# Block 1's run-up reordered, values formed by units, memory halves behind the turns

## The chip, the cores and the metric

The kernel runs on one core of a Trainium2 chip. The metric is the device time of one execution in microseconds (us), as the median of several runs.

## The reference

Two transformer blocks of two layers each work on one sequence of 256 tokens of width 1024, in float32. Cut to what matters here:

```
block 1, layer l (SWA = sliding window with sinks, DSA = sparse attention by an index):
  h = x @ w_in; qa,ka,va,qb,kb,vb,qi,ki,wi = split(h)     # 8 heads of 64; index: 8 heads of 32
  rope(qa, ka, qb, kb, qi); ki = rope(layer_norm(ki))
  idx = sum_h relu(qi_h . ki) * wi_h, causal; sel = top_k(idx, 64)
  oa = softmax(qa.ka/8 in a band of 128, with a sink) @ va
  ob = softmax(qb.kb/8 over sel and causal) @ vb
  x = layer_norm(a*x + [oa,ob] @ w_o); then a gated FFN with an extra input p, and a layer norm
block 2, layer l (MLA = latent attention, SLC = selected, WIN = window, with a compressed branch):
  three sets of causal attention, 8 heads each; x = layer_norm(a*x + mix @ w_out)
  cross attention with memory: k, v = (norm(mem) @ wkv) split; then a convolved FFN, layer norm
```

## The kernel before

The kernel is written by hand: each engine has one list of instructions (its queue), and semaphores make one wait for another. Tokens are two tiles of 128 (t = 0, 1). Big products are made from weights split in a high and a low part (ScalarE copies `whi`, L1348; VectorE, here DVE, subtracts to `wlo`, L1736) and three TensorE (PE) matmuls (L742 to L744). `token_stage` (PE) and `evict` (ScalarE) run a projection pass by pass: pass (q, t) is weight tile q for token tile t, and a dictionary names work that is put ahead of a pass (`before`) or behind one (`behind`).

In block 1 the input projection has seven weight tiles. Between its passes stand the turns (transposes through PE) of the index heads (`first_heads`), the index scores of tile 0 (`first_scores`, L1039), and on DVE the rotations (`rope`, L1800 to L1805) and the weighted sum of the index scores (`index_sum`, L2031) of rectified scores (ScalarE, L1519). GpSimd (POOL) rotates tile 0 of the window heads (L2421 to L2430). Behind the projection PE makes the index scores of tile 1, the turns of head groups 2 to 7 (`head_turns`, L1031), evicted by ScalarE (`heads_out`, L1509), and `attention` begins.

The sparse selection finds the 64 largest of a row in 8 rounds of 8 (`MAX8` L2111 and `MATCH_REPLACE8` L2113), for tile 0 on 128 columns and for tile 1 on 256, then builds a mask (L2116, L2118). DVE's function `top` makes these in the first six steps of attention.

`attention` works in steps i over half units. A unit is one kind of attention for one token tile, a half unit four of its heads. Block 1 has 4 units (8 half units, 11 steps): SWA t0, SWA t1, DSA t0, DSA t1. Block 2 has 6 (12 half units, 15 steps): MLA t0, t1, SLC t0, WIN t0, SLC t1, WIN t1. In step i:

- PE: the scores of half unit i (L898); a filler of block 2; a memory half, if step i is a slot (`SLOTS1`, `SLOTS2`); the values of half unit i-3 (L927, wait for `pt_ready`); the turns of the probabilities of half unit i-2 (L944, wait for `prob_ready`).
- DVE: mask and maximum of i (L1822, the CUSTOM rows, to L1835); the reciprocal for i-1 (L1847); `top(i)`; in even steps the low part of a finished unit's mix (L1861).
- ScalarE (ACT): in even steps the high part of the mix (L1437), the exponentials of i (L1452), the store of the step's memory half (`memory_store`, L1424), the evictions of the turned probabilities of i-2 (L1468), and in `HI_STEPS` a weight split.
- POOL: probabilities of half unit i-1 times the reciprocals (L2403).

A memory half (`memory_half`, L874 or L876) is 8 float32 matmul pairs of a product that block 2's cross attention needs later. It uses one PSUM bank, so each waits for the store of the one before (`kv_staged`). Six halves stand in each attention. When the second half of a tile is done, its room in the ring of weights is free, and the SyncE queue (SP) issues the next weight load.

Of the kernel before, what the change touches and what calls it, by code (L numbers as in the profile page):

```python
# [11 lines left out]
ALU = mybir.AluOpType  # L12
# [3 lines left out]
P = 128  # L16
S = 256
NT = S // P
# [29 lines left out]
SLOTS1 = (1, 2, 3, 5, 7, 9)  # L48
# [177 lines left out]
def build(nc, w, c, out):  # L226
# [52 lines left out]
    with ExitStack() as ctx:  # L279
# [124 lines left out]
        icomb_done = sem("icomb_done")  # L404
# [76 lines left out]
        relu = sy[:, 1, :].rearrange("p (h k) -> p h k", h=H)  # L481
# [173 lines left out]
        head_groups = [(10, 11), (12,), (5, 6), (7, 8), (9,), (0, 1), (2, 3), (4,)]  # L655
        n_const_dmas, n_param_dmas = len(const_dmas), len(param_dmas)
# [77 lines left out]
        def _(pe):  # L734
# [143 lines left out]

            def memory_between(n, banks):

                for half in range(2):
                    memory_half(n + half, banks[:, 2 + half, 0:TC])

            def attention(block, l, qT, kT, v, first_values=lambda t: None, filler=lambda step: None):
# [3 lines left out]
                for i in range(first, first + count + 3):  # L888
# [15 lines left out]
                    n = memory_slot(block, l, i - first)  # L904
                    if n is not None:
                        if n:
                            pe.wait_ge(kv_staged, n)
                        memory_half(n)
                    if half_ahead:
                        filler(i - first)  # L910
                    if i - 3 >= first:
                        n = i - 3
# [20 lines left out]
                    if first <= i - 2 < first + count:  # L933
# [5 lines left out]
                        for q, (b, a, kb) in enumerate(blk):  # L939
# [6 lines left out]
                            if q % 4 == 3:  # L946
                                ins.then_inc(pt_done, 1)

# [61 lines left out]
            for l in range(L):  # L1010
# [16 lines left out]
                def head_turns(q):  # L1027

                    for j, b in enumerate(head_groups[q]):
                        for t in range(NT):  # L1030
                            ins = pe.transpose((psa if q < 2 else psw)[:, q % 4, j * S + t * P:j * S + (t + 1) * P],  # L1031
# [40 lines left out]

                def bank_free(g, t):
                    if g < 2:
                        pe.wait_ge(pp_ready, 4 * l + 2 * t + g + 1)
                    else:
# [5 lines left out]
                             (6, 0): first_scores})  # L1082
                pe.wait_ge(relu_done, NT * l + 1)
                index_scores(1)

                pe.wait_ge(proj_ready, 8 * (l + 1))
                for q in range(2, 8):
                    if q == 2:
                        pe.wait_ge(qkb_roped, NT * (l + 1))
                    if q == 5:  # L1090
                        for t in range(NT):
                            pe.wait_ge(qka_roped[t], l + 1)
                    if q >= 6:
                        pe.wait_ge(heads_ready, 8 * l + q - 3)
                    head_turns(q)
                pe.wait_ge(heads_ready, 8 * (l + 1))
                pe.wait_ge(relu_done, NT * (l + 1))
# [1388 lines left out]
```

## Time and profile before

| | us |
|---|---|
| median of 3 runs | 1553.19 (1549.77 to 1553.95) |
| the profiled execution's own time | 1555.47 |
| its span | 1553.7 |
| busy: PE / PE weight load / DVE / ACT / POOL | 1497.1 / 1264.5 / 1063.1 / 778.6 / 123.3 |
| block 1's attention with its head turns, layers 0 and 1 | about 67 to 122 and 400 to 454 |
| block 2's attention, layers 0 and 1 | about 769 to 834 and 1199 to 1262 |

The profile is of one execution. Busy time is the time in which an engine had work in flight; matmuls are pipelined, so a busy PE need not be PE at its peak. All times of rows count from the start of the span.

### The profile page before, as it was taken

The numbers are of one execution on the slowest core, as the hardware profiler recorded it, in microseconds if no ns is written. First come the engines' busy times: TensorE is split into PE (matmuls) and PEld (weight loads), VectorE is DVE, ScalarE is ACT, GpSimd is POOL, SyncE is SP. The second block draws the span as 40 slices with busy tenths as digits, with TensorE's granted clock in tenths as the row PEclk, the third lists the DMA queues.
The fourth block names the chain that finished last, engine by engine and source line by source line (L and its number), as shares of the span: only waits on it lengthen the run. The fifth ranks groups of instructions, "written<-read, shape, count | busy, mean of one in ns | idle before, by whom it ended". The sixth has DMA issues, their size and how long they took to land.

```text
span 1553.7 us, 21682 instructions
## 1 busy us (share of the span) xinstructions
PE 1497.1 (96%) x8433; PEld 1264.5 (81%) x8433; DVE 1063.1 (68%) x1713; ACT 778.6 (50%) x1162; POOL 123.3 (8%) x98
## 2 busy tenths in 40 slices
PE   8989999999899999999999999999999999999997
PEld 5767888888777888878877988888788779888886
DVE  7767588667866787676345566878864455677777
ACT  4564444434464444433655344666545653446563
POOL 0130000000220000011022000000010320000000
PEclk9999999999999999999999999999999999999999
DMA  7624655655334755654614745556536147355551
GB/s 257 199 99 139 201 192 190 211 179 192 117 120 155 242 192 188 219 173 135 190 59 151 252 134 171 185 189 217 175 122 193 53 150 258 125 168 185 189 189 67
DMA packets 184429, 265.03 MB, mean 171 GB/s; under 512 B 7368, under 2 KB 139398, under 8 KB 184200
## 3 DMA queue, kind: packets, MB, share of 16 engines
q1 hardware_dynamic: 178712, 258.38, 50.1%
q10 hardware_dynamic: 5616, 5.26, 1.0%
q8 instruction: 68, 1.11, 0.3%
q14 instruction: 33, 0.27, 0.1%
HBM read 258.38 MB, written 5.24 MB: 170 GB/s over the span
## 4 chain that ended last, share of the span: by engine, by line
PE 77%; DVE 13%; ACT 5%; issue 2%; DVEq 2%; POOL 1%; ACTq 0%; POOLq 0%; DMA 0%; SPq 0%
PE psw L815 18%; PE psw L814 8%; PE psw L742 8%; PE psw L744 7%; PE psw L743 7%; DVE wlo L1736 5%; PE psa L742 4%; PE psa L744 4%; PE psa L743 4%; PE psa L874 3%; PE psa L876 3%; PE psa L927 2%; PE psw L898 2%; ACT sy L1452 1%; PE psa L944 1%
## 5 line engine op out<-in xcount | busy, mean ns | idle before, releaser
L1736 DVE TENSOR_TENSOR wlo<-raw,whi 128x2048 fp32r<-128x2048 f32 (+3 forms) x199 | 449.9, 2266 | 125.0 <-ACT whi L1348 124.5
L815 PE MATMUL psw<-xboth,whi 128*128 128x512 f32 x1344 | 464.8, 396 | 1.2 <-DVE wlo L1736 1.2
L1348 ACT ACTIVATE whi<-raw 128x2048 fp32r<-128x2048 f32 (+3 forms) x199 | 375.2, 1886 | 175.8 <-PE psw L744 91.3
L814 PE MATMUL psw<-xboth,wlo 128*128 128x256 f32 x1176 | 327.9, 279 | 0.0
L815 PEld LDWEIGHTS psw<-xboth,whi 128*128 128x128 f32 x1344 | 242.7, 188 | 49.1 <-DVE wlo L1736 2.3
L814 PEld LDWEIGHTS psw<-xboth,wlo 128*128 128x128 f32 x1176 | 221.7, 189 | 7.5
L742 PE MATMUL psw<-whi,xboth 128*128 128x512 f32 (+3 forms) x472 | 182.1, 386 | 5.3 <-DVE wlo L1736 5.3
L744 PE MATMUL psw<-whi,xboth 128*128 128x512 f32 (+3 forms) x472 | 178.9, 379 | 0.0
L743 PE MATMUL psw<-wlo,xboth 128*128 128x512 f32 (+3 forms) x472 | 178.9, 379 | 0.0
L1410 ACT ACTIVATE r<-psw 128x512 f32<-128x512 f32 x88 | 52.5, 596 | 174.6 <-PE psw L815 164.0
L742 PE MATMUL psa<-whi,rr 128*128 128x512 f32 x352 | 137.5, 391 | 1.4 <-DVE rr L2366 1.4
L743 PE MATMUL psa<-wlo,rr 128*128 128x512 f32 x352 | 137.0, 389 | 0.0
L2391 POOL TENSOR_TENSOR rstd<-vare,mhalf 128x1 f32<-128x1 f32 x26 | 36.7, 1414 | 1095.6 <-DVE vare L1758 1086.9
L2345 DVE SCALAR_TENSOR_TENSOR r<-r,pcol 128x254 f32<-128x254 f32 (+1 forms) x176 | 77.3, 481 | 57.9 <-ACT r L1702 53.9
L742 PEld LDWEIGHTS psw<-whi,xboth 128*128 128x128 f32 x472 | 88.9, 188 | 22.3 <-DVE wlo L1736 6.3
L744 PEld LDWEIGHTS psw<-whi,xboth 128*128 128x128 f32 x472 | 88.9, 188 | 15.9
L743 PEld LDWEIGHTS psw<-wlo,xboth 128*128 128x128 f32 x472 | 88.9, 188 | 15.2 <-issue 0.2
L744 PE MATMUL psa<-whi,rr 128*128 128x512 f32 x256 | 99.6, 389 | 0.0
L1903 DVE TENSOR_TENSOR r<-psw,r 128x512 f32<-128x512 f32 x88 | 60.6, 688 | 57.0 <-ACT r L1410 56.9
L1452 ACT ACTIVATE sy<-sy,nmx 128x256 f32<-128x256 f32 (+1 forms) x160 | 70.6, 446 | 22.9 <-DVE nmx L1835 22.8
L1702 ACT ACTIVATE r<-r,pcol 128x256 f32<-128x256 f32 x88 | 48.2, 596 | 67.3 <-DVE r L1903 67.3
L2403 POOL TENSOR_TENSOR sy<-sy,rden 128x512 f32<-128x512 f32 (+1 forms) x40 | 62.8, 1570 | 210.7 <-DVE rden L1847 169.8
(290 smaller groups left out, 2210.1 us busy)
## 6 DMA issues: line engine op xcount, KB each, us to landing
raw<-in_w_gu SPq DMA_DIRECT2D x44, 1024.0 KB, 5.1
raw<-in_ffn_w_up SPq DMA_DIRECT2D x42, 1024.0 KB, 5.1
raw<-in_w_down SPq DMA_DIRECT2D x22, 1024.0 KB, 4.9
raw<-in_ffn_w_down SPq DMA_DIRECT2D x22, 1024.0 KB, 4.9
raw<-in_w_in SPq DMA_DIRECT2D x20, 1024.0 KB, 5.3
raw<-in_xa_wkv SPq DMA_DIRECT2D x16, 1024.0 KB, 5.3
raw<-in_w_o SPq DMA_DIRECT2D x8, 1024.0 KB, 5.1
raw<-in_w_out SPq DMA_DIRECT2D x8, 1024.0 KB, 5.2
```

The source lines that it names most:

```text
L742: pe.matmul(o, lh, rh, start=first, stop=False)
L743: pe.matmul(o, lh, rl, start=False, stop=False)
L744: return pe.matmul(o, ll, rh, start=False, stop=last)
L814: pe.matmul(bank[:, 0:S], wl[:, k, cols], xhi[:, k, :], start=False, stop=False)
L815: ins = pe.matmul(bank.rearrange("p (i s) -> p i s", i=2), wh[:, k, cols], xboth[:, :, k, :], start=k == 0, stop=k == KD - 1)
L1348: nc.scalar.activation(tile_flat("hi", i), tile_flat("raw", i), ACT.Copy).then_inc(hi_ready, 1)
L1410: nc.scalar.activation(low_part[:, i], psw[:, 2 * i:2 * i + 2, S:2 * S], ACT.Copy).then_inc(low_out, 1)
L1452: ins = nc.scalar.activation(soft[:, u % 2, h, 0:nk], soft[:, u % 2, h, 0:nk], ACT.Exp, bias=nmx[:, u % 2, h:h + 1], scale=1.0, accum_out= ...
L1736: v.tensor_tensor(tile_flat("lo", i), tile_flat("raw", i), tile_flat("hi", i).bitcast(F32), ALU.subtract).then_inc(lo_ready, 1)
L1903: v.tensor_tensor((gsum, usum)[i].rearrange("p (c s) -> p c s", c=2), psw[:, 2 * i:2 * i + 2, 0:S], low_part[:, i], ALU.add).then_inc(ffn_ ...
L2345: ins = v.scalar_tensor_tensor(out=o, in0=whole[:, ch * S:(ch + 1) * S - lag], scalar=pcol[:, 1 + 2 * l, cc:cc + 1], in1=o, op0=ALU.mult, ...
L2403: g.tensor_tensor(x, x, rd.unsqueeze(3).broadcast_to([P, 2, 2, nk]), ALU.mult).then_inc(prob_ready, 1)
```

## The change

- The index scores go one pass earlier: those of tile 0 ahead of pass (5, 1), those of tile 1 (`second_scores`) ahead of pass (6, 0), into a rectified buffer of their own in `cblocks`; ScalarE's `rectified` moves with them.
- Behind the projection PE turns head groups 2 to 4, makes memory half 0 of the layer (slot -1), and then turns groups 5 to 7. ScalarE stores that half between the evictions of groups 4 and 5. The turns use other banks (`head_banks`).
- DVE makes four of tile 0's eight selection rounds ahead of attention: two behind the sum of tile 0, two behind the sum of tile 1. `TOP_STEPS` spreads the rest evenly over steps 0 to 5.
- In both blocks the values of both half units of a unit stand together in an even step (i-4 and i-3), where the first stood one step earlier.
- In both blocks a step's memory half stands behind the turns of the step, where it stood ahead of the values; step 1 of block 2 stays as it was. ScalarE stores it behind its evictions.

```diff
-SLOTS1 = (1, 2, 3, 5, 7, 9)
+SLOTS1 = (-1, 1, 3, 5, 7, 9)
+TOP_FIRST = 4
+TOP_STEPS = {0: (0, 4, 6), 1: (0, 6, 8), 2: (1, 0, 2), 3: (1, 2, 4), 4: (1, 4, 6), 5: (1, 6, 8)}
...
+        relus = [sy[:, 1, :].rearrange("p (h k) -> p h k", h=H), cblocks[:, 0:2048].rearrange("p (h k) -> p h k", h=H)]
...
+        head_banks = [(psa, 0), (psa, 1), (psw, 0), (psw, 2), (psw, 1), (psw, 3), (psa, 0), (psa, 1)]
...
+            def half_in_step(n):
+
+                if n:
+                    pe.wait_ge(kv_staged, n)
+                memory_half(n)
...
                     half_ahead = block == 2 and i - first == SLOTS2[0]
                     if not half_ahead:
                         filler(i - first)
-                    n = memory_slot(block, l, i - first)
-                    if n is not None:
-                        if n:
-                            pe.wait_ge(kv_staged, n)
-                        memory_half(n)
+                    half_now = memory_slot(block, l, i - first)
                     if half_ahead:
+                        half_in_step(half_now)
                         filler(i - first)
-                    if i - 3 >= first:
-                        n = i - 3
+                    for n in (i - 4, i - 3) if i % 2 == 0 and i - 4 >= first else ():
                         u, hf = divmod(n, 2)
...
+                    if not half_ahead and half_now is not None:
+                        half_in_step(half_now)
...
+                def second_scores():
+                    pe.wait_ge(relu_done, NT * l + 1)
+                    index_scores(1)
...
                 token_stage(1, "in", l, 7, x_in, 3, 0, bank_free,
                             {(2, 0): lambda: norm_turns(x_in, 1), (3, 0): param_turns,
                              (4, 0): memory_turns, (5, 0): first_heads,
-                             (6, 0): first_scores})
-                pe.wait_ge(relu_done, NT * l + 1)
-                index_scores(1)
-
+                             (5, 1): first_scores, (6, 0): second_scores})
+
+                pe.wait_ge(qkb_roped, NT * (l + 1))
+                for q in range(2, 5):
+                    pe.wait_ge(proj_ready, 8 * l + q + 3)
+                    head_turns(q)
+                pe.wait_ge(relu_done, NT * (l + 1))
+                memory_half(FIRST_HALF[1, l])
                 pe.wait_ge(proj_ready, 8 * (l + 1))
-                for q in range(2, 8):
-                    if q == 2:
-                        pe.wait_ge(qkb_roped, NT * (l + 1))
-                    if q == 5:
-                        for t in range(NT):
-                            pe.wait_ge(qka_roped[t], l + 1)
-                    if q >= 6:
-                        pe.wait_ge(heads_ready, 8 * l + q - 3)
+                for t in range(NT):
+                    pe.wait_ge(qka_roped[t], l + 1)
+                for q in range(5, 8):
                     head_turns(q)
                 pe.wait_ge(heads_ready, 8 * (l + 1))
-                pe.wait_ge(relu_done, NT * (l + 1))
...
                     filler(i - first)
-                    half = memory_slot(block, l, i - first)
-                    if half is not None:
-                        memory_store(half, stage[block - 1][:, half % 2, :])
                     if first <= i - 2 < first + count:
                         n = i - 2
                         for m in range(chunk0[n], chunk0[n + 1]):
@@ -1466,6 +1472,9 @@
                                 owner = max(x for x in range(len(chunk0) - 1) if chunk0[x] <= m - 4)
                                 act.wait_ge(pv_done, owner + 1)
                             nc.scalar.activation(pt[:, m % 4, :], psa[:, m % 2, :], ACT.Copy).then_inc(pt_ready, 1)
+                    half = memory_slot(block, l, i - first)
+                    if half is not None:
+                        memory_store(half, stage[block - 1][:, half % 2, :])
                     if i - first in HI_STEPS[block]:
                         serve(memory_key(block, l, HI_STEPS[block].index(i - first)))
...
-                evict(1, "in", l, 7, 3, proj_out, {(1, 0): second_tokens},
-                      {(2, 1): params_out, (3, 1): memory_out, (4, 1): first_heads_out, (5, 1): lambda: rectified(0)})
-                rectified(1)
+                evict(1, "in", l, 7, 3, proj_out,
+                      {(1, 0): second_tokens, (5, 1): lambda: rectified(0), (6, 0): lambda: rectified(1)},
+                      {(2, 1): params_out, (3, 1): memory_out, (4, 1): first_heads_out})
                 for q in range(2, 8):
                     heads_out(q)
+                    if q == 4:
+                        memory_store(FIRST_HALF[1, l], stage[0][:, 0, :])
                 attention(1, l)
...
+
+                def top_rounds(t, r0, r1):
+
+                    nk = (t + 1) * P
+                    sc = iscore[:, t, 0:nk]
+                    for _ in range(r0, r1):
+                        v.max(out=top8[:], in_=sc)
+                        dve.drain()
+                        v.match_replace(out=sc, in_to_replace=top8[:], in_values=sc, imm_value=TAKEN)
+                        dve.drain()
+                    if r1 == TOPK // 8:
+                        v.tensor_scalar(dmask[:, t, 0:nk], sc, TAKEN / 2, MASKED, ALU.is_gt, ALU.mult)
+                        dve.drain()
+                        v.tensor_tensor(dmask[:, t, 0:nk], dmask[:, t, 0:nk], causal[:, S - nk:S], ALU.add)
+                        dve.drain()
...
                     if q == 5:
                         index_sum(0)
+                        top_rounds(0, 0, 2)
...
                 index_sum(1)
-                dve.drain()
+                top_rounds(0, 2, TOP_FIRST)
 
                 def top(step):
 
-                    if step >= 6:
-                        return
-                    t, part_ = divmod(step, 3)
-                    nk = (t + 1) * P
-                    sc = iscore[:, t, 0:nk]
-                    for _ in range((part_ + 1) * (TOPK // 8) // 3 - part_ * (TOPK // 8) // 3):
-                        v.max(out=top8[:], in_=sc)
-                        dve.drain()
-                        v.match_replace(out=sc, in_to_replace=top8[:], in_values=sc, imm_value=TAKEN)
-                        dve.drain()
-                    if part_ == 2:
-                        v.tensor_scalar(dmask[:, t, 0:nk], sc, TAKEN / 2, MASKED, ALU.is_gt, ALU.mult)
-                        dve.drain()
-                        v.tensor_tensor(dmask[:, t, 0:nk], dmask[:, t, 0:nk], causal[:, S - nk:S], ALU.add)
-                        dve.drain()
+                    if step in TOP_STEPS:
+                        top_rounds(*TOP_STEPS[step])
```

## Rows read from the trace of the kernel before

**Rows 1.** The page: busy us (share of the span) and instructions by engine.
```profile
PE 1497.1 (96%) x8433; PEld 1264.5 (81%) x8433; DVE 1063.1 (68%) x1713; ACT 778.6 (50%) x1162; POOL 123.3 (8%) x98
```

**Rows 2.** Who PE waited for, whole span: us in total, times, longest.
```profile
PE psa L927 <- ACT pt L1468: 8.3, 11, 1.2
PE psa L874 <- ACT r L1424: 6.1, 2, 3.0
PE psw L742 <- DVE wlo L1736: 5.3, 4, 1.5
```

**Rows 3.** Stretches: length, busy us (instructions) by engine, granted clock, DMA share, GB/s.
```profile
67.00:122.00 55.00, 47.65 (x334) 37.31 (x327) 38.79 (x162) 36.08 (x103) 11.77 (x8) 0.94 0.32 106
...
400.00:454.00 54.00, 46.53 (x338) 36.56 (x331) 39.08 (x163) 35.89 (x103) 11.77 (x8) 0.97 0.32 107
...
768.00:834.00 66.00, 61.38 (x488) 49.40 (x487) 30.95 (x147) 44.72 (x135) 19.63 (x12) 0.97 0.27 88
...
1198.00:1262.00 64.00, 59.38 (x485) 47.94 (x485) 31.00 (x147) 44.31 (x134) 19.63 (x12) 1.00 0.27 91
```

**Rows 4.** Timeline of PE, block 1: start, us, what, [idle before, released by].
```profile
66.10 1.15 PE L1039 MATMUL psa<-r 32*128 32x256 f32 x16
...
69.44 1.41 PE L1031 MATMUL psw<-ident,r 128*128 128x128 f32 x10 [0.94 <-DVE r L1805]
71.94 1.16 PE L898 MATMUL psw<-r 64*128 64x128 f32 x16 [1.09 <-ACT r L1509]
73.03 3.72 PE L874 MATMUL psa<-memT,raw 128*128 128x256 f32 x16
...
80.85 6.49 PE L874 MATMUL psa<-memT,raw 128*128 128x256 f32 x16 [3.03 <-ACT r L1424]
...
104.25 1.09 PE L927 MATMUL psa<-pt,r 128*64 128x128 f32 x16 [0.72 <-ACT pt L1468]
...
120.43 1.09 PE L927 MATMUL psa<-pt,r 128*64 128x128 f32 x16 [0.74 <-ACT pt L1468]
...
414.12 5.41 PE L874 MATMUL psa<-memT,raw 128*128 128x256 f32 x16 [3.03 <-ACT r L1424]
```

**Rows 5.** Timeline of DVE, layer 0 of block 1.
```profile
66.69 0.83 DVE L1800 TENSOR_TENSOR sy<-r,cos 128x640 f32<-128x640 f32 x1 [1.77 <-ACT r L1546]
...
73.95 0.29 DVE L1822 CUSTOM_DVE_ANT_0 sy<-psw,band 128x128 f32<-128x128 f32 x1
...
75.27 0.16 DVE L1835 TENSOR_SCALAR nmx<-mx 128x4 f32<-128x4 f32 x1
...
79.75 0.29 DVE L2111 MAX8 top<-r 128x8 f32<-128x128 f32 x1
...
80.54 0.29 DVE L2111 MAX8 top<-r 128x8 f32<-128x128 f32 x1
...
81.38 0.42 DVE L1822 CUSTOM_DVE_ANT_0 sy<-psw,band 128x256 f32<-128x256 f32 x1
...
83.64 0.26 DVE L2111 MAX8 top<-r 128x8 f32<-128x128 f32 x1
```

**Rows 6.** Timeline of POOL, layer 0 of block 1.
```profile
79.15 1.04 POOL L2403 TENSOR_TENSOR sy<-sy,rden 128x512 f32<-128x512 f32 x1 [13.44 <-DVE rden L1847]
...
91.30 1.90 POOL L2403 TENSOR_TENSOR sy<-sy,rden 128x1024 f32<-128x1024 f32 x1 [6.46 <-DVE rden L1847]
```

**Rows 7.** Timeline of ACT, late in the attention of layer 0, block 1.
```profile
112.35 1.90 ACT L1348 ACTIVATE whi<-raw 128x2048 fp32r<-128x2048 f32 x1
114.63 1.09 ACT L1468 ACTIVATE pt<-psa 128x512 f32<-128x512 f32 x2
```

**Rows 8.** Timeline of PE, layer 0 of block 2.
```profile
781.43 2.57 PE L898 MATMUL psw<-r 96*128 96x256 f32 x8
...
824.38 1.09 PE L927 MATMUL psa<-pt,r 128*64 128x128 f32 x16 [1.21 <-ACT pt L1468]
```

**Rows 9.** Timeline of DVE, layer 1 of block 1, beside POOL's rotation.
```profile
390.88 1.87 DVE L1800 TENSOR_TENSOR sy<-r,cos 128x576 f32<-128x576 f32 x1
```

More of the change, by code:

```diff
@@ L403, in build @@
         relu_done = sem("relu_done")
-        icomb_done = sem("icomb_done")
         scores_done = sem("scores_done")
@@ L1027, in head_turns @@
                 def head_turns(q):
+                    bank, place = head_banks[q]
                     for j, b in enumerate(head_groups[q]):
                         for t in range(NT):
-                            ins = pe.transpose((psa if q < 2 else psw)[:, q % 4, j * S + t * P:j * S + (t + 1) * P],
+                            ins = pe.transpose(bank[:, place, j * S + t * P:j * S + (t + 1) * P],
                                                roped[:, t, b * P:(b + 1) * P], ident[:])
@@ L1509, in heads_out @@
                     nc.scalar.activation(headT[:, grp[0]:grp[0] + nb, :],
-                                         bank2(psa if q < 2 else psw, q % 4)[:, 0:nb, :], ACT.Copy).then_inc(heads_ready, 1)
+                                         bank2(*head_banks[q])[:, 0:nb, :], ACT.Copy).then_inc(heads_ready, 1)
                 def rectified(t):
@@ L1515, in rectified @@
                     act.wait_ge(iscores_done, NT * l + t + 1)
-                    if t == 1:
-                        act.wait_ge(icomb_done, NT * l + 1)
                     for j in range(4):
-                        ins = nc.scalar.activation(relu[:, j:8:4, 0:nk], bank2(psa, j)[:, :, 0:nk], ACT.Relu)
+                        ins = nc.scalar.activation(relus[t][:, j:8:4, 0:nk], bank2(psa, j)[:, :, 0:nk], ACT.Relu)
                     ins.then_inc(relu_done, 1)
@@ L2030, in index_sum @@
                     for h in range(H):
-                        ins = v.scalar_tensor_tensor(out=sc, in0=relu[:, h, 0:nk], scalar=wi_s[:, t, h:h + 1],
-                                                     in1=cm if h == 0 else sc, op0=ALU.mult, op1=ALU.add)
-                        if h < H - 1:
-                            dve.drain()
-                    ins.then_inc(icomb_done, 1)
+                        v.scalar_tensor_tensor(out=sc, in0=relus[t][:, h, 0:nk], scalar=wi_s[:, t, h:h + 1],
+                                               in1=cm if h == 0 else sc, op0=ALU.mult, op1=ALU.add)
+                        dve.drain()
[11 more added lines that the diff above has]
+                        v.tensor_tensor(dmask[:, t, 0:nk], dmask[:, t, 0:nk], causal[:, S - nk:S], ALU.add)
+                        dve.drain()
                 t1 = sy[:, 0, 0:640]
@@ L2100, in _ @@
                 index_sum(1)
-                dve.drain()
+                top_rounds(0, 2, TOP_FIRST)
                 def top(step):
-                    if step >= 6:
-                        return
-                    t, part_ = divmod(step, 3)
-                    nk = (t + 1) * P
-                    sc = iscore[:, t, 0:nk]
-                    for _ in range((part_ + 1) * (TOPK // 8) // 3 - part_ * (TOPK // 8) // 3):
-                        v.max(out=top8[:], in_=sc)
-                        dve.drain()
-                        v.match_replace(out=sc, in_to_replace=top8[:], in_values=sc, imm_value=TAKEN)
-                        dve.drain()
-                    if part_ == 2:
-                        v.tensor_scalar(dmask[:, t, 0:nk], sc, TAKEN / 2, MASKED, ALU.is_gt, ALU.mult)
-                        dve.drain()
-                        v.tensor_tensor(dmask[:, t, 0:nk], dmask[:, t, 0:nk], causal[:, S - nk:S], ALU.add)
-                        dve.drain()
+                    if step in TOP_STEPS:
+                        top_rounds(*TOP_STEPS[step])
                 def mask(kind, h, t):
```

1 line of the change is left out of this document (removed).

## The prediction

> **What bounds the kernel now.** I read the page's busy table first: TensorE (PE) is busy 96% of the span and no other engine above 68% [rows 1], so only what stops or slows PE can move the end. The view of who PE waited for comes next. Two of its largest lines are touched by the change: matmuls of values (L927) waiting for ScalarE's evictions of turned probabilities, 8.3 us in 11 waits, and the memory half (L874) waiting for the staged store of the half before it, 6.1 us in 2 [rows 2]. The table by stretches says where: block 1's two attention stages (67 to 122 and 400 to 454) hold 55 - 47.65 = 7.35 and 54 - 46.53 = 7.47 us without PE; block 2's two hold 4.6 each [rows 3]. These 24 us are all that the change can win by filling, plus what the clock costs: half 1 of layer 0 took 6.49 us after an idle 3.03, half 0 before it 3.72; in layer 1 half 1 took 5.41 [rows 4]. So 2.8 and 1.7 us were lost to the lower of the clock's two levels (1.2 GHz instead of 2.4; mean granted clock 0.94 and 0.97 there, [rows 3]). All sums below are differences within the profiled execution, 1555.47 us (span 1553.7), and are added to the median of the runs, 1553.19, which lies 0.15% under it.
>
> **1. The run-up of block 1.** Both index scores move one pass of PE earlier. PE's sum stays, but the last pass, and with it the eviction that DVE's rotation of tile 1 waits for (idle 1.77 us at 66.69, [rows 5]), comes later by the index scores of tile 1, some 1.1 us (they ran from 66.10 to 67.18, just behind the pass; now they stand ahead of it). DVE fills its wait in layer 0 with two rounds of the selection; a round on 128 columns is 80.54 - 79.75 = 0.79 us [rows 5], so 1.6 us, hidden. In layer 1 DVE had no wait there, so the 1.6 us stand on its path, in place of the 1.1. Then rotation 2.6, sum of tile 1 (4.4 us), both as before, and two more rounds, 1.6. The first mask and maximum (73.95 before) starts at 73.95 + 1.0 + 1.6 = about 76.4 in layer 0, and some 3.0 later than now in layer 1.
>
> PE meanwhile: turns of groups 2 to 4 (1.3 us), memory half 0 (3.66), turns 5 to 7 (1.25). Started at 67.1 they end at 73.3; ScalarE's last eviction is behind them and the first scores start near 73.95, where they started at 71.94 [rows 4]. Half 0 covers the 0.94 us for the rotation, about 0.6 us remain of the 1.09 before the scores. PE is 2.0 us later at the scores and has 3.7 us less to do behind them: 1.65 won. In layer 1: 407.3 against 405.2, 1.55 won.
>
> **2. The first half units.** This is where it is paid back. Half 1 no longer waits for a store, so 3.03 us of idle go [rows 4]. PE runs scores 0 and 1, half 1 (to 78.95) and scores 2 (to 80.0), and then meets the turns of half unit 0, which now nothing covers. DVE's order gives their time: mask and maximum 1.5 (73.95 to 75.43), two rounds 1.6, the next maximum 1.5, the reciprocal 0.3, GpSimd's product 1.04 [rows 5, 6], with a hop of 0.06 at each hand-over. 76.4 + 1.5 + 1.6 + 1.5 + 0.3 + 1.1 = 82.4: PE waits 2.5 us (2.95 in layer 1). Scores 3 end at 84.1. For the turns of half unit 1 DVE needs two rounds and the mask (2.2), the maximum on 256 columns with the reciprocal (81.38 to 83.64, 2.3), and GpSimd again 1.1: 87.0, PE waits 2.9. Before, halves 1 and 2 stood ahead of these turns and hid both. The turns of half unit 3 wait another 1.4: two rounds on 256 columns (2.1) between two maxima, then the product of 1.90 [rows 6], and half 3 queued behind them instead of in front. Last, the turns of half unit 7 wait 1.6 us for ScalarE's evictions of 6 (1.09 for two, [rows 7]), because ScalarE now stores half 4 behind its evictions, and then makes a weight split of 1.90 [rows 7] and the mix copy first. The values of half unit 1 wait 0.4.
>
> Idle behind the first scores in layer 0: 2.5 + 2.9 + 0.4 + 1.4 + 1.6 = 8.8 us. Before it was 7.35 [rows 3] less the 0.94 and 1.09 ahead of them [rows 4] = 5.3, with 2.8 lost to the clock. Net: -1.65 + 8.8 - 5.3 - 2.8 = -1.0. In layer 1: -1.55 + 9.3 - 5.3 - 1.7 = +0.8.
>
> **3. Values by units.** The same matmuls (16 take 1.09, [rows 4]), no added work. Both halves of a unit stand behind the scores of an even step, so the later evictions have a half or a step of scores in front: the 0.72 at 104.25 and the 0.74 at 120.43 go [rows 4]. They are counted in the sum above. The mix copy can start no earlier, since it waited for the later half before as well.
>
> **4. Block 2.** The same two reorderings, step 1 excepted. By the same chain in layer 1, the waits of values that I expect to go are 0.2, 0.5, 1.2 (the 1.21 of [rows 8]) and 0.74; those that come are turns 1 (0.7), turns 3 (0.5), turns 9 (1.4: a split and the mix copy on ScalarE delay their exponentials, and half 4 now stands behind them), turns 11 (0.3) and values 5 (0.8). The wait of 1.04 for the compressed branch stays and grows by nothing, since half 1 is stored 0.4 us behind its end, under 0.64 us of scores. Sum -2.6 + 3.7 = +1.1; I take +0.75, since the same working gives the stage before 1 us too long. Layer 0 differs by a fall of the clock around 780 (eight matmuls of scores took 2.57 us at 781.43, [rows 8], 0.7 more than the same in layer 1), which overlaps the waits: +0.1.
>
> **5. Moved halves and the queues behind them.** Half 3 ends 0.4 us later in step 5 and half 5 ends 2.0 us ahead of the output projection, not 3.8. SP's next weight load and ScalarE's split hang on that. The projection's first two passes need nothing of it for 5 us, and the split is 1.90: cost nothing. If that cover is gone, PE meets a split that is late, 1 to 1.5 us a time as at 4 places now (5.3 in 4, [rows 2]). GpSimd's rotation of tile 0 now runs beside DVE's sum of tile 0 and its two new rounds. Lower end: nothing, as the round at 79.75 beside the product at 79.15 [rows 5, 6]. Upper end: a product of DVE's own rotation beside it took 1.87 for 576 columns, where 640 took 0.83 alone [rows 5, 9]; if the part that overlaps slows like that, +1 us in layer 1, and nothing in layer 0, which has slack up to 67.7. The rounds are nearest to the rounds: 0.
>
> **6. The clock.** In block 1 PE now stands still 2.5 and 2.9 us with one set of scores between. Before, one idle spell of 3.03 was enough for the lower level in both layers [rows 4]. Half 2 comes behind these waits; at the lower level all through it would take 2.8 more. Some of it is absorbed, because the later wait for the turns of half unit 3 (1.4) and the 0.4 shrink by as much. Ends per layer: 0 and 2.3 (2.8 + 0.9 of other matmuls - 1.4). Where the clock comes back is what decides; the two cases before lost 2.8 and 1.7 of PE's time, less 1.4 absorbed is 1.4 and 0.3, mean 0.8: taken, 1.6 for both. The Trainium skill (TensorE: Matmul & The Clock Gate, Part 1) says it as "the default state is throttled, and activity releases the throttle". By that the release comes only from the work behind the second wait, which is half 2 itself, and the cost would be nearer 2.3 a layer. Its result is the first rival.
>
> **Sum.** -1.0 + 0.8 + 0.1 + 0.75 + 1.6 = +2.3 us, 0.15%: 1555.5.
>
> **Rivals.**
> *A, slower through the clock.* PE stays at the lower level through half 2 in both layers: 2.3 each instead of 0.8, so 2.3 + 3.0 = +5.3: 1558.5. For it: one wait of 3 us did it twice [rows 4]. Against: PE has 12 us of dense work ahead of the first wait, where it had 6. It decides at the start of half 2 near 88.
> *B, faster.* The halves behind the turns cost nothing: the probabilities are there when PE comes, as when DVE's and ScalarE's steps are shorter than I chain them, or PE reaches the turns later. The point is whether GpSimd's product of half unit n ends before scores n+2. Then the waits at turns 3 and 7 in block 1 (3.0 a layer) and those at turns 1, 3, 9 in block 2 (2.6 a layer) fall away, 11.2 us in all, of which I leave 2 for waits that then come elsewhere: 1546. For it: in the steady part before, turns never waited for GpSimd. Against: halves stood ahead of them then.
> *C, the clock never falls* in the four stages: -1.0 + 0.8 + 0.75 - 1.3 (the fall at 780 goes as well) = -0.8: 1552.
> *D, the tail.* The splits behind half 5 come late at the projection: 4 waits of 1.2: 1560.
>
> **Chances.** Forecast 0.42 (its own range 1552 to 1558), A 0.22, B 0.18, C 0.10, D 0.08. A measurement of this kernel can tell about 0.3%, 4.7 us, from no change, so faster is under 1548.5 and slower above 1557.9. Faster takes B and a little more: 0.21. Slower takes A, less its part under the bound, D and the forecast's upper end: 0.27. The same: 0.52. The range leaves out the far half of B and of D: 1548.5 to 1560.
>
> **What would show it.** Step 1: the first mask and maximum of layer 0 2.5 us behind 73.95, first scores 2 us behind 71.94, memory half ahead of them at full speed. Step 2: no wait of L874 for L1424; in its place L944 waiting for GpSimd's L2403, twice 2.5 to 3 us a layer of block 1. Step 3: L927's 8.3 us down to under 2. Step 4: block 2's stages longer by under 1 us. Step 6: granted clock under 0.9 around 84 to 92. I am wrong if L944's new waits come to under 5 us in the whole trace (then B), or if a stretch outside the four stages changes by over 1 us.

## The result: 1557.3 us, 0.27% slower, and the profile after

The changed kernel takes 1557.32 us (median of 6 runs, 1553.37 to 1557.91), the kernel before 1553.14 in the same comparison (6 runs, 1549.77 to 1553.95): ratio 1.0027, 95% interval 1.0015 to 1.0039. That is 4.2 us more, where 2.3 were forecast. The profiled execution took 1557.86 us, its span is 1556.1 (before 1553.7, so +2.4 in the two traces). PE's busy time fell by 6.0 us [rows 1], so more than that was added in waiting:

```profile
PE 1491.1 (96%) x8433; PEld 1262.7 (81%) x8433; DVE 1064.3 (68%) x1713; ACT 777.8 (50%) x1162; POOL 122.5 (8%) x98
```

Who PE waited for after the change (us in total, times, longest), to be held against [rows 2]:

```profile
PE psa L948 <- ACT pt L1474: 13.0, 10, 2.0
PE psa L948 <- POOL sy L2413: 10.2, 4, 3.1
PE psw L744 <- DVE wlo L1745: 5.3, 4, 1.5
...
PE psa L931 <- ACT pt L1474: 0.3, 2, 0.2
```

The two old waits are gone: values (L927, now L931) wait 0.3 us instead of 8.3, and no memory half waits for a store. In their place the turns (L948) wait 13.0 + 10.2 = 23.2 us. The splits behind the stage (`wlo`) wait as before.

To see where it fell I cut both traces at the same instructions: from the turns of head group 2 (block 1) or the first scores (block 2) to the first matmul of the output projection. Each number is a difference of two start times in PE's timeline.

| attention of | before | after | measured | forecast |
|---|---|---|---|---|
| block 1, layer 0 | 54.27 | 56.82 | +2.55 | -0.2 (-1.0, and 0.8 for the clock) |
| block 1, layer 1 | 53.19 | 56.02 | +2.83 | +1.6 (+0.8, and 0.8 for the clock) |
| block 2, layer 0 | 64.39 | 62.17 | -2.22 | +0.1 |
| block 2, layer 1 | 62.75 | 62.17 | -0.58 | +0.75 |
| all the rest | 1319.1 | 1318.9 | -0.2 | 0 |

The total came out near the forecast because two errors cancel, and that is luck: block 1 lost 5.4 us where 1.4 were forecast, block 2 won 2.8 where a loss of 0.85 was forecast. PE's timeline of block 1 shows the first, beside [rows 4]:

```profile
74.46 1.16 PE L906 MATMUL psw<-r 64*128 64x128 f32 x16 [1.15 <-ACT r L1518]
75.55 3.72 PE L876 MATMUL psa<-memT,raw 128*128 128x256 f32 x16
79.20 1.13 PE L906 MATMUL psw<-r 64*128 64x256 f32 x8
83.04 0.93 PE L948 MATMUL psa<-ident,sy 128*128 128x128 f32 x4 [2.70 <-POOL sy L2413]
83.89 2.08 PE L906 MATMUL psw<-r 64*128 64x256 f32 x8
87.56 1.12 PE L948 MATMUL psa<-ident,sy 128*128 128x128 f32 x4 [1.58 <-POOL sy L2413]
88.46 6.12 PE L876 MATMUL psa<-memT,raw 128*128 128x256 f32 x16
...
116.29 1.06 PE L948 MATMUL psa<-ident,sy 128*128 128x128 f32 x8 [2.01 <-ACT pt L1474]
117.19 5.31 PE L876 MATMUL psa<-memT,raw 128*128 128x256 f32 x16
```

and of layer 1:

```profile
424.49 5.31 PE L878 MATMUL psa<-raw,memT 128*128 128x256 f32 x16
...
452.86 4.85 PE L878 MATMUL psa<-raw,memT 128*128 128x256 f32 x16
```

The first waits stand at their forecast places (turns at 83.0 and 87.6; forecast 82.4 and 87.0). But the half behind them takes 6.12 and 5.31 us instead of 3.62, and the last half (behind a wait of 2.0 in both layers) 5.31 and 4.85. The same 16 matmuls take 3.62 elsewhere in the same trace. The windows say what differs; columns are those of [rows 3], the last three being granted clock, DMA share and GB/s:

```profile
67.50:85.10 17.60, 13.74 (x88) 11.29 (x88) 14.64 (x64) 8.53 (x28) 1.04 (x1) 0.95 0.39 135
85.10:103.60 18.50, 15.79 (x92) 12.33 (x88) 13.88 (x70) 11.38 (x42) 5.87 (x4) 0.77 0.03 8
103.60:124.30 20.70, 18.69 (x152) 15.12 (x152) 9.40 (x25) 13.69 (x30) 4.83 (x3) 0.92 0.37 117
```

Cut finer, the granted clock of layer 0 was 0.50 from 83.5 to 93.5, from the turns behind the first wait until well into half 2, and 1.00 from 94. In layer 1 it fell only behind the second wait, at about 424.6, and was back at 428.5. Few bytes moved during the slow half (DMA share 0.03 and 0.06), so transfers do not explain it.

In block 2, layer 1 (no slow scores in either trace) PE's groups of instructions, with busy us, mean ns, and idle time before them, are, before:

```profile
L876 PE MATMUL psa<-raw,memT 128*128 128x256 f32 x96 | 22.0, 382 | 1.0 <-ACT cblocks L1655 1.0
L927 PE MATMUL psa<-pt,r 128*64 128x128 f32 x144 | 10.5, 281 | 2.2 <-ACT pt L1468 1.9
L944 PE MATMUL psa<-ident,sy 128*128 128x128 f32 x72 | 10.4, 281 | 0.0
```

and after:

```profile
L878 PE MATMUL psa<-raw,memT 128*128 128x256 f32 x96 | 21.7, 379 | 0.0
L948 PE MATMUL psa<-ident,sy 128*128 128x128 f32 x72 | 10.3, 280 | 4.2 <-ACT pt L1474 3.3 <-issue 0.9
L931 PE MATMUL psa<-pt,r 128*64 128x128 f32 x144 | 9.4, 278 | 0.2 <-ACT pt L1474 0.2
```

Waits rise by 1.0 (3.4, with 0.2 of the values' filler, to 4.4), as forecast (+1.1). But the same 144 matmuls of values take 9.4 us of PE instead of 10.5: 32 in a row take 1.97 where two groups of 16 took 1.09 each (why is not shown: a lead-in of each group that a neighbour of the same kind covers would do it, but no run isolates that). With halves and turns PE's busy time falls by 1.5 a layer, and the stage by 0.58 in spite of the waits. That term was missing from the forecast.

### The profile page after: what moved, and what is told of

Same layout as the page of the kernel before. It is cut to its first block, busy times and chain, and to the rows that moved or that the text cites. A ratio compares the mean times of both kernels' runs of the same rounds, so it can differ in the third digit from the quotient of the medians.

```text
span 1556.1 us, 21682 instructions
## 1 busy us (share of the span) xinstructions
PE 1491.1 (96%) x8433; PEld 1262.7 (81%) x8433; DVE 1064.3 (68%) x1713; ACT 777.8 (50%) x1162; POOL 122.5 (8%) x98
## 4 chain that ended last, share of the span: by engine, by line
PE 78%; DVE 11%; ACT 4%; issue 2%; DVEq 2%; POOL 1%; ACTq 0%; POOLq 0%; DMA 0%; SPq 0%
PE psw L817 18%; PE psw L744 8%; PE psw L816 8%; PE psw L746 8%; PE psw L745 8%; DVE wlo L1745 4%; PE psa L744 4%; PE psa L746 4%; PE psa L745 4%; PE psa L876 3%; PE psa L878 3%; PE psa L931 2%; PE psw L906 2%; POOL rstd L2401 1%; PE psa L948 1%
```

## The experiments

All times are medians of 12 runs (6 for e5 and e11, 11 for e7); ratios are to the kernel before in the same comparison, with 95% intervals. Before was 1553.19 to 1553.55 in the first, second and last group (e1 to e4, e5 to e8, e11 and e12) and 1552.77 in the third (e9, e10). Its runs lie in clusters near 1550.3, 1553.6 and 1555.8 us, so a difference of medians and one worked out from the ratios disagree by 1 to 1.5 us (e2: -2.3 and -1.1; e4: -1.6 and 0.0); differences below are of medians, and smaller than that they show nothing.

Stages are cut as above (block 1 layers 0 and 1, block 2 layers 0 and 1), each from one execution, which need not be a typical one: e3's lay 2.4 us under its median, e12's 4.1 over. Block 1 of e3 and of e4 has the same instructions and took 51.33 and 51.94 us in one trace, 54.22 and 53.42 in the other.

| kernel | us | ratio | stages |
|---|---|---|---|
| e1 run-up alone | 1555.76 | 1.0022 (1.0010 to 1.0034) | 52.70, 54.78, 64.33, 64.40 |
| e2 orders alone | 1550.90 | 0.9993 (0.9984 to 1.0002) | 53.51, 52.63, 62.18, 63.85 |
| e3 changed, halves ahead | 1549.35 | 0.9978 (0.9965 to 0.9990) | 51.33, 51.94, 60.54, 62.22 |
| e4 same, block 1 alone | 1551.59 | 1.0000 (0.9991 to 1.0010) | 54.22, 53.42, 62.18, 62.18 |
| e5 values by units alone | 1545.48 | 0.9950 (0.9937 to 0.9963) | 50.26, 51.65, 60.54, 62.19 |
| e6 changed, no early rounds | 1552.38 | 0.9994 (0.9984 to 1.0005) | 53.04, 52.97, 62.18, 62.18 |
| e7 e3, no early rounds | 1550.18 | 0.9985 (0.9976 to 0.9995) | 53.24, 52.73, 60.55, 62.21 |
| e8 changed, waits filled | 1551.50 | 0.9994 (0.9986 to 1.0003) | 52.73, 53.22, 62.18, 62.18 |
| e9 e5, half 0 early | 1552.76 | 0.9996 (0.9983 to 1.0009) | 54.72, 52.60, 62.13, 62.21 |
| e10 e3, waits filled | 1549.50 | 0.9984 (0.9972 to 0.9995) | 54.18, 53.40, 60.55, 62.19 |
| e11 e5, wait filled | 1544.05 | 0.9942 (0.9927 to 0.9957) | 50.62, 50.43, 63.75, 60.53 |
| e12 e3, half 0 back | 1548.25 | 0.9974 (0.9962 to 0.9986) | 53.36, 53.95, 62.12, 62.20 |

### The parts one by one

**e1**, the changed kernel with values and halves as before (the lines show what the edit comes to; the run's kernel says it with flags):

```diff
-                    for n in (i - 4, i - 3) if i % 2 == 0 and i - 4 >= first else ():
+                    half_in_step(half_now)      # where step i has one
+                    for n in (i - 3,) if i - 3 >= first else ():
```

> Only the new run-up of block 1; values and memory halves in both attentions as before. Stages are measured from the turns of head group 2 (block 1) or the first scores (block 2) to the first matmul of the output projection: before 54.3, 53.2, 64.4, 62.7 us; changed kernel 56.8, 56.0, 62.2, 62.2. Order theory (block 1 lost its 2.6 and 2.8 us because the halves stand behind the turns and uncover GpSimd's and ScalarE's steps, with the clock falling behind these waits): block 1's stages 51 to 53.5, block 2 as before, total about 1551. Run-up rival (the loss is DVE's path, 2.5 to 3 us later at the first maximum): block 1's stages stay at 56 to 57, total about 1558.

**e2**, the kernel before with both new orders (values by units, halves behind the turns, their stores behind the evictions):

```diff
-                    if i - 3 >= first:
-                        n = i - 3
+                    for n in (i - 4, i - 3) if i % 2 == 0 and i - 4 >= first else ():
...
+                    if not half_ahead and half_now is not None:
+                        half_in_step(half_now)
```

> Only the new order in both attentions (values by units, halves behind the turns); block 1's run-up as before, six halves in its attention. Order theory: block 1's stages above 54.3 and 53.2 by 1 to 4 each, block 2 at 62.2 each, total 1553 to 1558. Run-up rival: block 1's stages under 54, block 2 62.2, total about 1549.

**e3**, the changed kernel with each half ahead of values and turns and its store ahead of the evictions; **e4**, the same in block 1 alone.

```diff
+                    if front and not half_ahead and half_now is not None:
+                        half_in_step(half_now)
                     for n in (i - 4, i - 3) if i % 2 == 0 and i - 4 >= first else ():
...
-                    if not half_ahead and half_now is not None:
+                    if not front and not half_ahead and half_now is not None:
                         half_in_step(half_now)
```

> The changed kernel with the halves ahead of values and turns again in both attentions (values still by units, run-up still new). Order theory: no wait of the turns for GpSimd near 80 to 88, clock up, block 1's stages 51 to 53 each, block 2 61 to 64, total 1545 to 1550. Run-up rival: block 1's stages stay at 56, total 1556 or more.

> As the one before, but block 2 keeps its halves behind the turns. Block 1's stages as there. If the place of the halves is what won 2.2 us in block 2's layer 0, block 2's stages are 62.2 here and over 63 there, total 1 to 3 us under it; if values by units won it, both block 2 stages are the same or shorter there.

**e5**, the kernel before with values by units and nothing else:

```diff
-                    if i - 3 >= first:
-                        n = i - 3
+                    for n in (i - 4, i - 3) if i % 2 == 0 and i - 4 >= first else ():
```

> The kernel before with one edit: values are formed a unit at a time, both half units behind the scores of the even steps; run-up, memory halves and stores stay where they were. If the three parts add up (run-up +2.6 us, values by units -6.4, halves behind the turns +8.0, from the medians 1555.76, 1549.35 and 1557.32 against 1553.19), this is 1546.8 us, block 2's stages 60.6 us (were 64.4 and 62.75) and block 1's 52.9 and 50.4. If values by units helps only behind the new run-up, where PE waited for the eviction of a turn, it is 1551 to 1553 and only block 2 is shorter.

The order theory had put the whole loss on the halves' place; e1 (+2.6, where it wanted about -2) and e2 (-2.3, where it wanted 0 to +5) contradict it, and e3 and e4 give it back a part. Not the part it named, though: in e3 the turns of half unit 0 still wait 2.67 us for GpSimd in layer 0, and half 2 still takes 5.25. The question that e4 asked is decided for values by units: block 2's layer 0 is 60.54 with the halves ahead and 62.18 with them behind, so it is not their late place that made that stage 2.2 us shorter than before.

With e5 the change falls into three steps along one line: values by units 1553.2 to 1545.5 (-7.7), halves behind the turns to 1550.9 (+5.4), the new run-up to 1557.3 (+6.4). By the other line (run-up, units, halves) it is +2.6, -6.4, +8.0. So values by units wins and the two other parts lose, whatever the order in which they are added. With values by units in place, run-up and late halves cost 3.9 and 5.4 alone and 11.8 together, 2.5 more than their sum; by the ratios it is 0.9 more, so whether they make each other worse isn't settled. Halves behind the turns cost 62.18 - 60.54 = 1.64 us in a layer of block 2 (e4 against e3, layer 0), where I had priced 3.7 for all that comes there. Layer 1 hides it (62.18 and 62.22), because the clock fell there in e3's trace (0.50 from 1194 to 1197) and not in e4's.

### The clock

**e8**, the changed kernel with TensorE kept busy in two waits of block 1:

```diff
+                        if block == 1 and n - first in FILL:          # FILL = {0: 20, 1: 12}
+                            if chunk0[n] >= 2:
+                                pe.wait_ge(pt_ready, chunk0[n] - 1)
+                            for _ in range(FILL[n - first]):
+                                pe.transpose(psa[:, chunk0[n] % 2, 0:P], ident[:], ident[:])
                         pe.wait_ge(prob_ready, n + 1)
```

> The changed kernel with idle TensorE time filled: ahead of its wait for the probabilities of half unit 0 of block 1 it turns the identity 20 times into the bank that the turns then overwrite (about 2.6 us, the wait being 2.7 and 3.1), and 12 times ahead of half unit 1 (1.5 us, waits 1.6 and 2.9). If it is the clock that makes half 2 take 6.12 and 5.31 us, it takes 3.62 to 4 in both layers, block 1's stages lose 1 to 2 us each (part goes into longer waits behind it) and the time is 1554 to 1555.5. Rival: half 2 is slowed by something else (its operands, the store of half 1), stays above 5 us, and the time is 1557 or more.

PE's timeline of layer 0 in e8 (the probabilities come no earlier; half 2 is at 87.50, half 5 at 114.24):

```profile
79.72 2.40 PE L946 MATMUL psa<-ident 128*128 128x128 f32 x20
82.48 0.66 PE L954 MATMUL psa<-ident,sy 128*128 128x128 f32 x4 [0.36 <-POOL sy L2419]
83.06 1.14 PE L907 MATMUL psw<-r 64*128 64x256 f32 x8
84.13 1.53 PE L946 MATMUL psa<-ident 128*128 128x128 f32 x12
87.00 0.66 PE L954 MATMUL psa<-ident,sy 128*128 128x128 f32 x4 [1.34 <-POOL sy L2419]
87.50 3.62 PE L877 MATMUL psa<-memT,raw 128*128 128x256 f32 x16
...
113.34 1.06 PE L954 MATMUL psa<-ident,sy 128*128 128x128 f32 x8 [2.02 <-ACT pt L1480]
114.24 3.62 PE L877 MATMUL psa<-memT,raw 128*128 128x256 f32 x16
```

and the windows over its two stages of block 1:

```profile
66.00:120.00 54.00, 47.70 (x367) 39.51 (x366) 37.91 (x156) 33.85 (x100) 12.11 (x9) 1.00 0.28 92
398.00:453.00 55.00, 48.21 (x369) 39.92 (x368) 39.29 (x163) 34.48 (x101) 12.21 (x9) 1.00 0.28 94
```

32 more instructions a layer, work that nobody needs, make the kernel 5.8 us faster (5.1 by the ratios). The clock is 1.00 in both stages, half 2 takes 3.62, scores 3 1.14 instead of 2.08. Half 5 is back at full speed as well (3.62 at 114.24) although its wait of 2.0 is still there. The stages are 4.1 and 2.8 us shorter, twice what I expected. Up to the last turns the two layers win 2.4 and 1.1 us (half 2), and from there to the end 1.7 each (half 5, which nobody filled for). It is the lower level of 1.2 GHz that made the halves slow, and nothing in their operands.

**e11**, e5 with its wait of 3.0 us ahead of half 1 filled in the same way:

```diff
+                    if block == 1 and i - first == 2:
+                        if chunk0[first] >= 2:
+                            pe.wait_ge(pt_ready, chunk0[first] - 1)
+                        for _ in range(20):
+                            pe.transpose(psa[:, chunk0[first] % 2, 0:P], ident[:], ident[:])
                     if front and not half_ahead and half_now is not None:
                         half_in_step(half_now)
```

> The kernel before with values by units (1545.48) and its wait of 3.0 us ahead of half 1 of block 1 filled with 20 turns of the identity (2.4 us). There half 1 took 3.72 us in layer 0 and 5.41 in layer 1, behind the same wait. If the clock is what makes the 5.41, it takes 3.72 in both layers and the time is 1544 (1.7 us of one layer, less what goes into a wait behind it). Rival: the fill starts late or the half is late by it, nothing is won: 1545.5 or more.

It has the lowest median of all: 9.5 us under the kernel before, 1.4 under e5 (the two intervals overlap, so that it beats e5 is not shown). Half 1 behaved as expected. PE in layer 1, e5 and then e11:

```profile
410.05 5.41 PE L875 MATMUL psa<-memT,raw 128*128 128x256 f32 x16 [3.02 <-ACT r L1432]
```

```profile
406.75 2.40 PE L920 MATMUL psa<-ident 128*128 128x128 f32 x20
409.85 3.72 PE L875 MATMUL psa<-memT,raw 128*128 128x256 f32 x16 [0.70 <-ACT r L1437]
```

**e10**, the same filling as in e8 put into e3.

> The changed kernel with memory halves ahead of values and turns (1549.35), and its idle time ahead of the first two turns of block 1 filled with turns of the identity as in the run before. With the clock held up half 2 takes 3.62 to 3.72 instead of 5.25, and the time is 1547 to 1548; the second filling stands behind half 2 here, where PE hardly waited, and may cost 0.5 to 1.5 us a layer. If the new run-up costs nothing but the clock, it comes to the 1545.5 of the kernel before with values by units; if DVE's path costs as well, it stays 1.5 to 3 above.

Nothing was won. Half 2 took 3.72, but PE then reached the values before ScalarE had evicted the turns, and the clock fell there:

```profile
93.56 1.12 PE L941 MATMUL psa<-pt,r 128*64 128x128 f32 x8 [2.60 <-ACT pt L1492]
94.62 1.97 PE L963 MATMUL psa<-ident,sy 128*128 128x128 f32 x8
96.52 1.23 PE L909 MATMUL psw<-r 64*128 64x128 f32 x8
97.67 4.68 PE L879 MATMUL psa<-memT,raw 128*128 128x256 f32 x16
```

### What in the run-up costs

**e6**, the changed kernel without the four early rounds (**e7**: the same in e3):

```diff
-TOP_STEPS = {0: (0, 4, 6), 1: (0, 6, 8), 2: (1, 0, 2), 3: (1, 2, 4), 4: (1, 4, 6), 5: (1, 6, 8)}
+TOP_STEPS = {0: (0, 0, 2), 1: (0, 2, 5), 2: (0, 5, 8), 3: (1, 0, 2), 4: (1, 2, 5), 5: (1, 5, 8)}
...
-                        top_rounds(0, 0, 2)
...
-                top_rounds(0, 2, TOP_FIRST)
```

> The changed kernel with no round of the selection ahead of attention: its 8 rounds of tile 0 stand in steps 0 to 2 and those of tile 1 in steps 3 to 5, as 2, 3, 3 each, as in the kernel before. If the four early rounds hold up the first maximum (3.2 us of DVE in layer 1, 1.6 in layer 0, where the first two fill a wait), the waits of 2.7 to 3.1 us for GpSimd at the turns of half unit 0 fall to 0.5 to 1.5 and block 1's stages to 54.5 to 55.5 us (are 56.8 and 56.0): 1554. Rival: steps 1 and 2 now have three rounds between two maxima (2.4 us), so the turns of half units 1 and 2 are late instead, and the time stays within 1 us of 1557.3.

> The changed kernel with both edits: memory halves ahead of values and turns, and no round ahead of attention. If the early rounds are what the run-up costs, 1549.35 less 2 to 3: 1546.5 us, with block 1's stages 49.5 to 50.5. Rival: halves ahead of the turns cover what the rounds leave, and it stays at 1549 to 1550.

e6 is 4.9 us faster, where 3.3 were expected, but only a part of that is DVE's path. In layer 0 the first wait for GpSimd fell from 2.70 to 1.26 us, the second rose to 2.93 (layer 1: 3.00), as its rival said, and half 2 was slow here too (5.31 and 4.53). Counted from the start of the stage, the second turns come 1.3 and 1.65 us earlier in the two layers, which is close to the price expected of the rounds. What is left of the 6.8 us between the two traces is nearly all the clock: half 5 was at full speed in both layers, 1.7 us each, behind nearly the same wait as in the changed kernel (layer 0):

```profile
114.15 1.06 PE L948 MATMUL psa<-ident,sy 128*128 128x128 f32 x8 [1.86 <-ACT pt L1474]
115.06 3.62 PE L876 MATMUL psa<-memT,raw 128*128 128x256 f32 x16
```

e7's time went the rival's way, but not for the rival's reason. The wait for GpSimd fell as in e6 (2.67 to 1.27 us in layer 0, against e3). With three rounds between two maxima the evictions of half unit 1 came late instead, and PE waited for them ahead of its values, 4.96 and 5.15 us where e3 waited 0.96 in layer 0:

```profile
92.45 1.12 PE L940 MATMUL psa<-pt,r 128*64 128x128 f32 x8 [4.96 <-ACT pt L1486]
```

**e9**, e5 with memory half 0 between head groups 4 and 5 (steps 2, 3, 5, 7, 9 for the others); **e12**, e3 with half 0 back in step 1. In both ScalarE's store of the half moves with it. First e9, then e12:

```diff
-SLOTS1 = (1, 2, 3, 5, 7, 9)
+SLOTS1 = (-1, 2, 3, 5, 7, 9)
...
                     head_turns(q)
+                    if q == 4:
+                        pe.wait_ge(relu_done, NT * (l + 1))
+                        memory_half(FIRST_HALF[1, l])
                 pe.wait_ge(heads_ready, 8 * (l + 1))
-                pe.wait_ge(relu_done, NT * (l + 1))
```

```diff
-SLOTS1 = (-1, 1, 3, 5, 7, 9)
+SLOTS1 = (1, 2, 3, 5, 7, 9)
...
-                memory_half(FIRST_HALF[1, l])
```

> The kernel before with values by units (1545.48) and one part of the new run-up alone: memory half 0 between the head turns of groups 4 and 5, the halves of block 1 in steps 2, 3, 5, 7, 9; index scores, the rotation of tile 1 and the selection stay as before. The theory: what the new run-up costs is DVE's path to the first maximum (the early rounds and the later last pass), not the moved half. Then the wait of 3.0 us at half 1 and 0.9 at the turns go (7.9 us in two layers), 3 to 5 of them come back as waits for the first maximum and for turns: 1541 to 1544.5. Rival: the moved half is itself what costs, since it only shifts idle time ahead of the first scores to behind them: 1545.5 to 1548.

> The changed kernel with halves ahead of values and turns (1549.35) and with memory half 0 taken out of the run-up again, back to step 1 (halves in steps 1, 2, 3, 5, 7, 9); index scores early, rotation of tile 1 and the four early rounds stay. If the moved half is what the new run-up costs, 1545 to 1546.5, as the kernel before with values by units. If the late last pass and the early rounds cost, since the first maximum stays 2 to 3 us behind, it is 1548 to 1550.5.

Here my theory fell. Moving the half, and nothing else, costs e9 7.3 us against e5. PE (e9, layer 0):

```profile
69.78 3.72 PE L875 MATMUL psa<-memT,raw 128*128 128x256 f32 x16 [0.94 <-ACT sy L1529]
73.33 1.26 PE L1039 MATMUL psw<-ident,r 128*128 128x128 f32 x10
75.75 1.16 PE L905 MATMUL psw<-r 64*128 64x128 f32 x16 [1.16 <-ACT r L1519]
...
88.47 6.33 PE L875 MATMUL psa<-memT,raw 128*128 128x256 f32 x16 [3.96 <-ACT r L1434]
```

and DVE's first maximum:

```profile
76.51 0.29 DVE L1834 CUSTOM_DVE_ANT_0 sy<-psw,band 128x128 f32<-128x128 f32 x1 [2.35 <-PE psw L905]
```

In the old run-up DVE is ready for the first scores at about 74; half 0 puts them off by 3.9 us (75.75, where e5 has 71.89), DVE stands still 2.35, and all that hangs on the maximum comes as much later. In the new run-up DVE is busy with sum and rounds until 76.7 anyway, so the half can hide behind it: e12, without the moved half, comes to within 1.1 us of e3, which the intervals don't tell apart. The moved half costs little there because DVE's path is slow already. What is left of the new run-up without it costs 2.8 us (e12 less e5; 3.7 by the ratios). No run takes the earlier index scores, the later last pass and the early rounds apart behind halves that stand ahead, so that DVE's path makes up these 2.8 is argued.

How the 7.3 divide stays open as well, but the late maximum is not all. The wait for a store moved from half 1 (3.00 us in e5) to half 2 (3.96), and half 2 took 6.33 us at the lower clock where e5 had 3.72. That is 2.6 of the 4.5 us by which block 1's layer 0 is longer. A further 1.6 lie in block 2, layer 0 (62.13 against 60.54), whose instructions are the same: the clock fell there in e9's trace (0.50 from 780 to 782) and not in e5's.

## Why the prediction was right, and where not

The time (1555.5, range 1548.5 to 1560) was 1.8 us low and inside the range, and "the same" is what came. The chain of waits was right. That the number came so near is luck, since a clock term 5.3 us too small is cancelled by a block 2 forecast 3.7 us too high and by 1.3 us too much for the waits of block 1. Point by point:

- **Step 1, the run-up: right.** First scores 0.5 us behind their forecast, the first maximum at 76.81 against 76.4, memory half 0 at full speed (3.62). The queues (step 5) cost nothing and rival D did not come: the stretches outside the four stages moved by 0.4 us at most, the waits for `wlo` by nothing.
- **Step 2, the new waits: right.** In layer 1 they are 3.06, 2.87, 1.13 and 2.01 where I had 2.95, 2.9, 1.4 and 1.6; in layer 0 the second is 1.58, since PE came slower. The 0.4 ahead of the values shows only in e8 (0.29 and 0.36). Without the clock (e8) the stages stand 1.5 us under before and level with it (53.22 against 53.19), where -1.0 and +0.8 were forecast. Rival C, no fall of the clock, was priced at 1552; e8, which makes it so by hand, took 1551.5.
- **Step 6, the clock: the direction right, the size wrong. This is the term that failed.** The sign it named came (granted clock 0.50 from 84 to 92). Taken at 0.8 a layer, the term was 4.1 and 2.8 (changed kernel less e8): 6.9 us against 1.6, or 5.8 by the medians.

  Half of it is half 2 (2.4 and 1.1 us). I had taken a mean of two earlier cases and let later waits absorb 1.4 of each. In layer 0 they absorbed nothing: the wait at the turns of half unit 3 is 1.13 us in the changed kernel and in e8 alike. There PE entered half 2 at the lower level, behind two waits close together, and the clock came back only in it, at 93.5. The half took 6.12 us, against 3.62 at the upper level and an estimated 7.2 (twice that) at the lower one throughout. The Trainium skill (TensorE: Matmul & The Clock Gate, Part 1) says that activity releases the throttle, and layer 0 agrees with it. The price of 2.8 "at the lower level all through" was too low by the same estimate, 3.6: the 6.49 us of [rows 4] were not all slow either, as the granted clock was 0.50 up to 86.0 and 1.00 from 86.5.

  The other half is half 5 (1.7 us in each layer): I listed the wait of 1.6 to 2.0 at the last turns and didn't ask what stood behind it.

  Rival A's time, 1558.5, is 1.2 us off the result, the forecast 1.8. A had the better mechanism for half 2, and 0.22 was too little for it, but it had nothing for half 5 and shared the forecast of block 2, so its nearness is luck too.
- **Steps 3 and 4, values by units: mis-sized, with the opposite sign.** "The same matmuls, no added work" overlooked that groups laid side by side take less of PE (10.5 to 9.4 us for 144). Values by units alone is worth 7.7 us (e5), about 2.2 of it in a quiet layer of block 2 (62.75 to 60.53 in e11). Not all is the order's own: of the 10.0 us between the stages of before and of e5, 4.4 are falls of the clock that only before's trace has (half 1 at 6.49, and block 2's layer 0), and e5 gives 1.7 back in block 2's layer 1. Before lost 1.6 us to the clock in block 2, layer 0 (eight scores at 2.57, [rows 8]; the forecast took 0.7), which the changed kernel did not (1.89 at 785.95). So the block 2 that should have lost 0.85 won 2.8.
- **Rival B** fell: the waits for GpSimd came to 10.2 us, not under 5. That e5 lies near its 1546 says nothing for it: e5 has the halves ahead and the old run-up.

## What to carry to other kernels

Change one order at a time: two losing edits (+5.4, +6.4) hid one that was worth 7.7 us. When a wait is priced, price the work behind it too, at both levels of the clock: where the clock fell, a wait of 2 to 3 us cost 1.2 to 2.5 us more in the 16 matmuls that followed. Compare stages of two traces only after looking at the granted clock in them: a fall in one of them, 1.6 us and more, is as large as most of the effects here. An early start for work that fills gaps helps only if the engine that sets the pace (here DVE's path to the first maximum) is not behind it.

## What was not expected of the hardware

Idle TensorE time filled with useless turns made the changed kernel faster, 5.8 us for 64 instructions; in e3 the same filling won nothing (e10). The lower clock level does not follow from one wait alone. Half 1 behind the same wait of 3.0 us took 3.72 us in layer 0 of e5 and 5.41 in layer 1. Half 5 behind a wait of 2.0 us took 5.31 and 4.85 in the changed kernel and 3.62 twice in e8. In e9, layer 1, the clock fell during the second of two waits of 1.15 and 1.14 with one set of scores between, and no longer wait stood near (in e11, layer 0, waits of 0.94 and 1.10 stood ahead of a fall after which half 0 took 4.40). The rows of e9:

```profile
409.47 1.16 PE L905 MATMUL psw<-r 64*128 64x128 f32 x16 [1.15 <-ACT r L1519]
411.77 2.08 PE L905 MATMUL psw<-r 64*128 64x256 f32 x8 [1.14 <-DVE nmx L1847]
413.78 5.81 PE L875 MATMUL psa<-memT,raw 128*128 128x256 f32 x16
```

A stage of one trace can be 1.7 us off another with the same instructions, as block 2's layer 1 is in e1 (64.40, with the clock at 0.50 from 1201 to 1203) and before (62.75, with none). Whether this is also why executions of one kernel scatter (before: 1549.8 to 1556.2 in 35 runs) is not shown. Only one execution of each kernel has a trace, and the mean granted clock of the runs does not order their times: before's fastest runs have 0.991 to 0.994, those near 1553.6 have 0.993 or 0.994, the slowest 0.990; e5's fastest have 0.994 and its slowest 0.997. When exactly the level falls stays open.
